# Summing the first experts' results: where the bias products, the residual rows and the last addition stand

## The chip, the cores and the metric

One core of one Trainium2 chip. The metric is the device time of a whole run in microseconds, as the median of several runs. All times inside a run are counted from the start of the profiled span.

## The reference

The program is two transformer blocks after one another on 512 tokens of width 1024. The first block ends in a mixture of 32 experts with 4 experts per token:

```python
y = act.astype(xb.dtype) @ w2[e] + b2[e]
...
out = jnp.zeros((T + 1, D), jnp.float32).at[buf_tok].add(ys.reshape(n_pad, D))[:T]
...
x = x + mod[:, 5] * moe_ffn(hf, *moe_w).reshape(B, L, D)
```

For each token: the four experts' outputs are multiplied by the token's gates and added, the experts' bias rows (`b_mlp2`) are added with the same gates, the sum is multiplied by a modulation row and added to the residual `x`. The second block starts from this `x`.

## The kernel before

A kernel is a chain of stages. Each stage (`stage(...)`) is a block in which the five engines run their own lists of instructions and meet at the end; the next stage begins when the last engine has arrived. Within a stage the order between engines is set by semaphores (`then_inc`, `wait_ge`).

The stage `combine1` is the function `combine`, called once by `expert_layer` after the first block's expert products. The 512 tokens are four tiles (`TX = 4`) of 128 tokens, one per partition, with 1024 columns. The work around the change:

- SyncE (SP) requests the 32 bias rows (`bias`, L2841), the modulation row on all partitions (`gate`, L2842), then the residual rows of the four tiles (`x_rows`, L2844), 128x1024 f32 each. In the kernel before they are requested at once, one after another.
- GpSimd (POOL) issues 16 gathers (L2851), tile by tile, four for each tile: gather j of tile t fetches, for every token of the tile, the output row of its j-th expert from `slot_rows` in HBM into `got[:, t, j]`. The first two of a tile count on `first[t]`, the last two on `rest[t]`.
- ScalarE turns gates into diagonal matrices (`shares`, L2880) and keeps the transposed gates (`spread_turned`, L2877).
- TensorE (PE) turns the gates (L2858). Then for each tile it multiplies them with the bias rows (L2864: two matmuls, shown as four instructions) and adds gathered rows 0 and 1 with the diagonal matrices (L2870: four matmuls, shown as eight instructions), all into two PSUM banks of the tile. All eight PSUM banks are in use, two for each tile. The last one signals `summed`.
- VectorE (DVE) adds gathered rows 2 and 3 (L2892, twice: the first reads PSUM, the second reads `total`), multiplies by `gate` (L2896) and adds the residual rows (L2898). `total` has two buffers, used in turn.

Behind it stands the stage `in2`, which begins with transposes of `x` on TensorE (L551), memsets on GpSimd (L3640) and the load of the first weights on SyncE (L147). The last stage of the program (`combine_last`, gathers at L2933, products at L2946) is built in the same way with two gathers for each tile and without residual rows.

Of the kernel before, what the change touches and what calls it, by code (L numbers as in the profile page):

```python
# [21 lines left out]
ALU = mybir.AluOpType  # L22
# [4 lines left out]
P = 128  # L27
D = 1024
DC = D // P
L = 512  # L30
LC = 256
TX = L // P
# [65 lines left out]
def record(**fields):  # L98

    return namedtuple("Record", list(fields))(**fields)  # L100
# [70 lines left out]
@contextmanager  # L171
def stage(core, name, *signals, pool_dma=(), from_one=()):

    nc = core.nc
    mine, other = core.halves[core.stages % 2], core.halves[1 - core.stages % 2]
    first = core.stages == 0
    core.stages += 1  # L180
    assert len(signals) <= len(mine)
    with ExitStack() as stack:  # L182
        found = {s: stack.enter_context(nc.semaphore(f"{name}_{s}", num=n)) for s, n in zip(signals, mine)}
        found.update({s: core.stack.enter_context(nc.semaphore(f"{name}_{s}")) for s in pool_dma})
        block = stack.enter_context(nc.Block(no_gpsimd_drain=True))
        if not first:
            @block.sync
            def _(sync):
                sync.sem_clear(range(other[0], other[-1] + 1))
        if from_one:  # L190
            @block.sync
            def _(sync):
                for signal in from_one:
                    sync.sem_inc(found[signal], 1)
        yield block, record(**found)


@contextmanager
def buffers(core, others=None, **shapes):

    with ExitStack() as stack:
        made = dict(others or {})
        for name, shape in shapes.items():
            kind = F32
            if not isinstance(shape[-1], int):
                *shape, kind = shape
            made[name] = stack.enter_context(core.nc.sbuf_tensor(f"{name}_{core.nc.next_id()}", list(shape), kind))
        yield record(**made)
# [24 lines left out]
def on_all(row, parts=P):  # L233

    return row.to_broadcast([parts, row.shape[1]])
# [2586 lines left out]
def combine(core, k, name, r, y_rows, rows, top, bias, x_rows):  # L2822

    psum = core.psum
    experts = bias.shape[0]
    by_tensor = top // 2
    with buffers(core, got=[P, TX, top, D], total=[P, 2, D], gate=[P, D], bias=[experts, D], spread_turned=[experts, L],
                 shares=[P, TX, by_tensor, P]) as b, \  # L2830
            stage(core, name, "gate_loaded", "added", "vector_step", "bias_loaded", "shares_turned", "shares_kept",
                  "spread_out", "summed", *[f"x{t}_loaded" for t in range(TX)],
                  pool_dma=("first0", "first1", "first2", "first3", "rest0", "rest1", "rest2", "rest3")) as (block, s):
        first = [s.first0, s.first1, s.first2, s.first3]
        rest = [s.rest0, s.rest1, s.rest2, s.rest3]
        sums_ps = psum[:, :, :].rearrange("p (t c) n -> p t (c n)", t=TX)
        x_loaded = [s.x0_loaded, s.x1_loaded, s.x2_loaded, s.x3_loaded]

        @block.sync
        def _(sync):  # L2840
            sync.dma_start(b.bias[:], bias).then_inc(s.bias_loaded, 16)  # L2841
            sync.dma_start(b.gate[:], on_all(rows[0:1, 5 * D:6 * D])).then_inc(s.gate_loaded, 16)  # L2842
            for t in range(TX):
                sync.dma_start(k.x[:, t], x_rows[t * P:(t + 1) * P, :]).then_inc(x_loaded[t], 16)  # L2844

        @block.gpsimd
        def _(pool):
            for t in range(TX):
                for j in range(top):
                    i = t * top + j  # L2850
                    pool.indirect_dma_start(b.got[:, t, j], None, y_rows,  # L2851
                                            bass.IndirectOffsetOnAxis(ap=r.dest[:, i:i + 1], axis=0))\
                        .then_inc(first[t] if j < by_tensor else rest[t], 16)

        @block.tensor
        def _(pe):
            for t in range(TX):
                mm = pe.transpose(psum[0:experts, 7, t * P:(t + 1) * P], r.shares[:, t, :], k.ident[:])  # L2858
            mm.then_inc(s.shares_turned, 1)
            pe.wait_ge(s.shares_kept, 1)  # L2860
            pe.wait_ge(s.bias_loaded, 16)
            for t in range(TX):
                for c in range(D // BANK):
                    pe.matmul(sums_ps[:, t, c * BANK:(c + 1) * BANK], b.spread_turned[:, t * P:(t + 1) * P],  # L2864
                              b.bias[:, c * BANK:(c + 1) * BANK], start=True, stop=False)
                pe.wait_ge(s.spread_out, t + 1)
                pe.wait_ge(first[t], 16 * by_tensor)
                for j in range(by_tensor):
                    for c in range(D // BANK):
                        mm = pe.matmul(sums_ps[:, t, c * BANK:(c + 1) * BANK], b.shares[:, t, j],  # L2870
                                       b.got[:, t, j, c * BANK:(c + 1) * BANK], start=False, stop=j == by_tensor - 1)
                mm.then_inc(s.summed, 1)

        @block.scalar
        def _(act):
            act.wait_ge(s.shares_turned, 1)
            act.copy(b.spread_turned[:], psum[0:experts, 7, :]).then_inc(s.shares_kept, 1)  # L2877
            for t in range(TX):
                for j in range(by_tensor):
                    ins = act.activation(b.shares[:, t, j], k.ident[:], ACT.Copy, scale=r.gates[:, t, j:j + 1])  # L2880
                ins.then_inc(s.spread_out, 1)
            act.wait_ge(s.spread_out, TX)

        @block.vector
        def _(dve):
            step = Steps(dve, s.vector_step)
            for t in range(TX):
                total = b.total[:, t % 2]
                dve.wait_ge(s.summed, t + 1)
                dve.wait_ge(rest[t], 16 * (top - by_tensor))  # L2890
                for j in range(by_tensor, top):
                    step(dve.scalar_tensor_tensor(out=total, in0=b.got[:, t, j], scalar=r.gates[:, t, j:j + 1],  # L2892
                                                  in1=sums_ps[:, t] if j == by_tensor else total, op0=ALU.mult, op1=ALU.add))
                if t == 0:
                    dve.wait_ge(s.gate_loaded, 16)
                step(dve.tensor_tensor(total, total, b.gate[:], ALU.mult))  # L2896
                dve.wait_ge(x_loaded[t], 16)
                dve.tensor_tensor(k.x[:, t], k.x[:, t], total, ALU.add).then_inc(s.added, 1)  # L2898
            dve.wait_ge(s.added, TX)


def combine_last(core, k, r, y_rows, gain, bias, out):
# [89 lines left out]
def expert_layer(core, k, args, which, router=None):  # L2992
# [13 lines left out]
    with buffers(core, logits=[P, TX, width], gates=[P, TX, top], dest=[P, TX * top, I32],  # L3006
# [39 lines left out]
        if first:  # L3046
            combine(core, k, "combine1", r, y_rows, k.rows1, top, args.b_mlp2[0], x_rows)
        else:
            combine_last(core, k, r, y_rows, args.ln2_g_2, args.ln2_b_2, args.out)
# [756 lines left out]
```

## Time and profile before

| | us |
|---|---|
| median of 3 runs | 2547.24 (2543.53 to 2547.29) |
| profiled execution, its own time | 2546.25 |
| span of the profiled execution | 2544.5 |
| mean granted TensorE clock | 0.909 |
| TensorE busy | 2161.3 (85%) |
| VectorE busy | 1025.3 (40%) |
| ScalarE busy | 734.6 (29%) |
| GpSimd busy | 268.7 (11%) |

Rows of the trace give times from the start of the span. `PE` is a matmul, `PEld` its weight load, `POOL` is GpSimd, `DVE` VectorE, `SP` SyncE; a row with xN merges N instructions of one line. The median and the span are not the same run: the profiled execution has its own time, 1.75 us above its span.

### The profile page before, as it was taken

To read this page: it belongs to the slowest core of one execution; us is meant where nothing else is said; L and a number is where in the kernel's file an instruction comes from. 1 tells how busy PE (TensorE), PEld (TensorE's weight loads), DVE (VectorE), ACT (ScalarE), POOL (GpSimd) and SP (SyncE) were. 2 spreads that over 40 slices of the span, in tenths; PEclk is the share of its full clock that TensorE was granted. 3 is DMA by queue.
4 is the path that set the end of the run, shared out by engine and by line. 5 is a ranking of instruction groups with operands and counts; after the bars stand their busy time and mean duration, and the time that the engine had idled before them with its cause. 6 is when DMAs were issued, how large, how long until landed. Compare 5 with 4: busy or idle time off the path is not lost. (4 is left out here: it accounts for less than half of the span.)

```text
span 2544.5 us, 43818 instructions
## 1 busy us (share of the span) xinstructions
PE 2161.3 (85%) x18094; PEld 1230.4 (48%) x18094; DVE 1025.3 (40%) x2002; ACT 734.6 (29%) x1874; POOL 268.7 (11%) x233
## 2 busy tenths in 40 slices
PE   5989779848998899889888887799989987793995
PEld 3965247733333344333333333488866644582442
DVE  3236546452222223222222221537246679545443
ACT  3223536321111111011101111235246677421322
POOL 0000000000000000000000000200059950000001
PEclk8999789969899999999999998899989996696997
DMA  6356620289799999999999995622000011302995
GB/s 237 109 205 251 253 90 1 77 362 416 306 421 421 420 421 419 420 421 420 421 421 420 420 410 237 251 85 83 34 2 1 1 68 67 141 17 88 418 418 199
DMA packets 147804, 628.05 MB, mean 247 GB/s; under 512 B 34516, under 2 KB 65492, under 8 KB 93848
## 3 DMA queue, kind: packets, MB, share of 16 engines
q1 hardware_dynamic: 118280, 575.56, 56.0%
q0 software_dynamic: 8064, 29.36, 2.9%
q10 hardware_dynamic: 21264, 20.34, 2.4%
q8 instruction: 143, 2.34, 0.4%
q14 instruction: 53, 0.43, 0.0%
HBM read 591.85 MB, written 33.38 MB: 246 GB/s over the span
## 5 line engine op out<-in xcount | busy, mean ns | idle before, releaser
L2292 PE MATMUL psum<-low,x 128*32 128x512 f32 x3520 | 416.9, 619 | 61.1 <-DMA low<-in_w_mlp 57.8
L2452 DVE TENSOR_TENSOR u<-psum,x 128x512 f32<-128x512 f32 x81 | 56.0, 691 | 690.9 <-PE psum L2292 690.9
L662 PE MATMUL psum<-high 128*128 128x512 f32 (+3 forms) x832 | 295.5, 355 | 19.2 <-DVE low L687 19.1
L662 PE MATMUL psum<-high,low 128*128 128x512 f32 (+3 forms) x832 | 293.3, 353 | 0.0
L662 PE MATMUL psum<-low,high 128*128 128x512 f32 (+3 forms) x832 | 293.2, 352 | 0.0
L2292 PEld LDWEIGHTS psum<-low,x 128*32 128x32 f32 x3520 | 113.4, 113 | 323.2 <-issue 234.3
L2301 PE MATMUL psum<-low,act_turned 128*32 128x256 f32 x4000 | 235.4, 387 | 3.9 <-DVE act_turned L2461 3.6
L2292 PE MATMUL psum<-high,x 128*32 128x512 f32 x1664 | 203.1, 628 | 37.2 <-DMA high<-in_w_mlp 31.9
L2301 PEld LDWEIGHTS psum<-low,act_turned 128*32 128x32 f32 x4000 | 132.7, 113 | 124.6 <-issue 51.8
L662 PEld LDWEIGHTS psum<-high 128*128 128x128 f32 x832 | 159.8, 192 | 42.4 <-issue 21.3
L2393 ACT ACTIVATE sig<-glu 128x256 f32<-128x256 f32 x81 | 34.5, 426 | 471.1 <-DVE glu L2453 470.8
L662 PEld LDWEIGHTS psum<-high,low 128*128 128x128 f32 x832 | 159.9, 192 | 21.4
L662 PEld LDWEIGHTS psum<-low,high 128*128 128x128 f32 x832 | 159.9, 192 | 20.9
L687 DVE TENSOR_TENSOR low<-weight_slots,high 128x1024 fp32r<-128x1024 f32 (+3 forms) x84 | 89.4, 1066 | 194.0 <-ACT high L681 193.3
L681 ACT CAST high<-weight_slots 128x1024 fp32r<-128x1024 f32 (+3 forms) x84 | 77.2, 920 | 216.1 <-PE psum L662 211.0
L2292 PEld LDWEIGHTS psum<-high,x 128*32 128x32 f32 x1664 | 52.8, 113 | 166.6 <-issue 113.2
L2384 ACT ACTIVATE x<-psum,cols,scale1f 128x128 f32<-128x128 f32 x160 | 58.0, 468 | 202.7 <-PE psum L2292 167.1
L2263 POOL DMA_INDIRECT x<-token_rows,slot_token x20 | 18.9, 946 | 889.8 <-PE psum L2283 868.6
L1229 ACT ACTIVATE weight_slots<-psum,shifts 128x768 f32<-128x768 f32 x96 | 86.6, 902 | 66.4 <-DVE shifts L1281 66.4
L355 PE MATMUL psum<-weight_slots,mix 128*32 128x512 f32 x384 | 58.9, 750 | 52.7 <-DMA weight_slots<-in_w_ada 28.4
L1280 DVE TENSOR_REDUCE peaks<-psum 128x1 f32<-128x768 f32 x96 | 91.5, 953 | 26.3 <-PE psum L1149 25.8
L2401 ACT COPY x<-psum 128x256 f32<-128x256 f32 x80 | 29.7, 372 | 239.2 <-DMA slot_rows<-x 149.5
(527 smaller groups left out, 3081.6 us busy)
## 6 DMA issues: line engine op xcount, KB each, us to landing
low<-in_w_mlp SPq DMA_DIRECT2D x141, 2048.0 KB, 27.2
high<-in_w_mlp SPq DMA_DIRECT2D x51, 2048.0 KB, 28.8
weight_slots<-in_w_ada SPq DMA_DIRECT2D x12, 2048.0 KB, 10.9
weight_slots<-in_w_mod SPq DMA_DIRECT2D x12, 2048.0 KB, 10.9
weight_slots<-in_w_in SPq DMA_DIRECT2D x8, 2048.0 KB, 8.4
gu<-in_w_gate SPq DMA_DIRECT2D x16, 1024.0 KB, 30.2
gu<-in_w_up SPq DMA_DIRECT2D x16, 1024.0 KB, 31.4
down<-in_w_down SPq DMA_DIRECT2D x16, 1024.0 KB, 31.4
```

Source lines behind the costliest of these rows:

```text
L355: mm = pe.matmul(out[c * 32:(c + 1) * 32], self.c[:, which, kp * self.KP + i, :], rows[:, i, c * BANK:(c + 1) * BANK], start=kp == 0 and i ...
L662: mm = pe.matmul(psum[:, p.group % 8, 0:p.width], *p.operands(x, weights[:, n % 2], u * QK_ + kc, kc), start=p.first and u == 0 and kc == ...
L681: act.copy(w.high[:, n % 2, :, 0:chunks[j].source.shape[2]], piece(j, u)).then_inc(s.high_made, 1)
L687: dve.tensor_tensor(w.low[at], piece(j, u), w.high[at].bitcast(F32), ALU.subtract).then_inc(s.low_made, 1)
L1229: act.activation(probs[c][:, t], rows_ps[t % 2], ACT.Exp, scale=scale, bias=b.shifts[:, c, t:t + 1], accum_out=b.sums[:, c, t:t + 1]).then ...
L1280: step(dve.tensor_reduce(b.peaks[:, c, t:t + 1], rows_ps[t % 2], AX, ALU.max))
L2292: mm = pe.matmul(psum[g * RB:(g + 1) * RB, bank, :], b.turned[:, kc, q * RB:(q + 1) * RB], w[:, i, g * BANK:(g + 1) * BANK], start=kc == 0 ...
L2301: mm = pe.matmul(psum[g * RB:(g + 1) * RB, 2 + parity, 0:YW], b.act_turned[:, parity, kc, :], w[:, i, g * YW:(g + 1) * YW], start=kc == 0, ...
L2384: ins = act.activation(b.turned[:, m, :], psum[:, 4 + m // 4, (m % 4) * P:(m % 4 + 1) * P], ACT.Identity, scale=k.scale1f[:, m:m + 1], bia ...
L2393: act.activation(b.sig[:], b.glu[:], ACT.Sigmoid, scale=ALPHA).then_inc(s.squashed, 1)
L2401: act.copy(b.y[:, q], psum[:, 2 + at % 2, 0:YW]).then_inc(s.y_kept, 1)
L2452: step.reach(dve.tensor_tensor(b.u[:], psum[:, bank, :], b.bias[:], ALU.add), s.biased, at + 1)
```

## The change

Three edits in `combine`. The bias products of all four tiles are issued before the first tile's gather products. SyncE requests the residual rows of tile t only when `rest[t]` has landed. The addition of `total` to the residual rows moves from VectorE to GpSimd, behind all its gathers; `total` gets a buffer for each tile, and a new semaphore, `totalled`, tells GpSimd that a tile's total is ready.

```diff
-    with buffers(core, got=[P, TX, top, D], total=[P, 2, D], gate=[P, D], bias=[experts, D], spread_turned=[experts, L],
+    with buffers(core, got=[P, TX, top, D], total=[P, TX, D], gate=[P, D], bias=[experts, D], spread_turned=[experts, L],
                  shares=[P, TX, by_tensor, P]) as b, \
-            stage(core, name, "gate_loaded", "added", "vector_step", "bias_loaded", "shares_turned", "shares_kept",
+            stage(core, name, "gate_loaded", "added", "totalled", "vector_step", "bias_loaded", "shares_turned", "shares_kept",
...
             for t in range(TX):
+
+                sync.wait_ge(rest[t], 16 * (top - by_tensor))
                 sync.dma_start(k.x[:, t], x_rows[t * P:(t + 1) * P, :]).then_inc(x_loaded[t], 16)
...
                         .then_inc(first[t] if j < by_tensor else rest[t], 16)
+            for t in range(TX):
+                pool.wait_ge(x_loaded[t], 16)
+                pool.wait_ge(s.totalled, t + 1)
+                pool.tensor_tensor(k.x[:, t], k.x[:, t], b.total[:, t], ALU.add).then_inc(s.added, 1)
+            pool.wait_ge(s.added, TX)
...
                     pe.matmul(sums_ps[:, t, c * BANK:(c + 1) * BANK], b.spread_turned[:, t * P:(t + 1) * P],
                               b.bias[:, c * BANK:(c + 1) * BANK], start=True, stop=False)
+            for t in range(TX):
                 pe.wait_ge(s.spread_out, t + 1)
                 pe.wait_ge(first[t], 16 * by_tensor)
...
-                total = b.total[:, t % 2]
+                total = b.total[:, t]
...
-                step(dve.tensor_tensor(total, total, b.gate[:], ALU.mult))
-                dve.wait_ge(x_loaded[t], 16)
-                dve.tensor_tensor(k.x[:, t], k.x[:, t], total, ALU.add).then_inc(s.added, 1)
-            dve.wait_ge(s.added, TX)
+                dve.tensor_tensor(total, total, b.gate[:], ALU.mult).then_inc(s.totalled, 1)
+            dve.wait_ge(s.totalled, TX)
```

## Rows read from the trace of the kernel before

**Rows 1.** The page, its first line.

```profile
span 2544.5 us, 43818 instructions
```

**Rows 2.** Timeline of the stage: start us, us, engine, line, instructions [idle before, releaser].

```profile
1586.50 0.94 POOL L2851 DMA_INDIRECT got<-slot_rows,dest  x1 [85.41 <-POOLq L182]
...
1588.37 3.75 PE L2864 MATMUL psum<-bias,spread_turned 32*128 32x512 f32 x4 [1.51 <-DMA bias<-in_b_mlp]
...
1597.30 5.66 PE L2870 MATMUL psum<-got,shares 128*128 128x512 f32 x8 [5.18 <-DMA got<-slot_rows,dest]
...
1602.89 1.98 PE L2864 MATMUL psum<-bias,spread_turned 32*128 32x512 f32 x4
...
1605.14 1.27 POOL L2851 DMA_INDIRECT got<-slot_rows,dest  x1 [0.30 <-issue]
...
1615.88 3.70 PE L2870 MATMUL psum<-got,shares 128*128 128x512 f32 x8
...
1619.62 1.28 DVE L2892 SCALAR_TENSOR_TENSOR total<-got,gates,psum 128x1024 f32<-128x1024 f32 x1 [0.42 <-PE psum L2870]
...
1623.51 1.23 DVE L2898 TENSOR_TENSOR x<-x,total 128x1024 f32<-128x1024 f32 x1
...
1625.34 3.53 PE L551 MATMUL psum<-ident,x 128*128 128x128 f32 x16 [5.76 <-PEq L182]
```

**Rows 3.** The same stage by line: duration ns min/median/max, first and last start us.

```profile
L2864 PE MATMUL psum<-bias,spread_turned x16: 587/588/1188, 1588.4 to 1615.4; 32*128 32x512 f32 x16
...
L2892 DVE SCALAR_TENSOR_TENSOR total<-got,gates,total x4: 1284/1284/1285, 1604.3 to 1620.9; 128x1024 f32<-128x1024 f32 x4
L2896 DVE TENSOR_TENSOR total<-total,gate x4: 1224/1224/1225, 1605.6 to 1622.3; 128x1024 f32<-128x1024 f32 x4
```

**Rows 4.** Windows of 2 us: busy us (count) by engine, PEclk, DMA share, GB/s.

```profile
1590.00:1592.00 2.00, 2.00 (x3) 0.33 (x1) 0.00 (x0) 0.00 (x0) 1.47 (x2) 0.50 1.00 381
...
1614.00:1616.00 2.00, 2.00 (x6) 0.75 (x6) 1.88 (x2) 0.00 (x0) 0.00 (x0) 1.00 0.83 330
```

**Rows 5.** DMA from 1580 to 1630: the gathers' queue, then issues (median us to landing).

```profile
q0 software_dynamic: 2304, 8.39, 42.1%
...
x<-x_rows SPq DMA_DIRECT2D x4, 512.0 KB, 9.0
...
bias<-in_b_mlp SPq DMA_DIRECT2D x1, 128.0 KB, 2.3
```

**Rows 6.** Landing of the gathers in this stage (L2851), then L2933 in the last stage.

```profile
DMA to landing us min/median/max: 8.1/11.6/11.8
...
L2933 POOL DMA_INDIRECT got<-slot_rows,dest x8: 936/938/941, 2510.9 to 2519.6; - x8
...
DMA to landing us min/median/max: 6.1/6.3/7.6
```

**Rows 7.** Windows of 1 us around a rise and a fall of the clock (columns as rows 4).

```profile
1600.00:1601.00 1.00, 1.00 (x3) 0.48 (x2) 0.00 (x0) 0.00 (x0) 0.84 (x1) 0.50 1.02 410
1601.00:1602.00 1.00, 1.00 (x4) 0.43 (x3) 0.00 (x0) 0.00 (x0) 0.69 (x2) 0.84 1.02 406
...
1621.00:1622.00 1.00, 0.00 (x0) 0.00 (x0) 1.00 (x1) 0.00 (x0) 0.00 (x0) 0.90 0.00 0
```

**Rows 8.** The gathers' queue from 2514 to 2515, last stage: packets, MB.

```profile
q0 software_dynamic: 28, 0.11, 30.9%
```

**Rows 9.** GpSimd's two-input operations, and VectorE's beside them: min/median/max ns.

```profile
L1109 POOL TENSOR_TENSOR acc<-acc,part x36: 1812/1832/1847, 1875.6 to 2050.6; 128x772 f32<-128x772 f32 x36
...
L3283 POOL TENSOR_TENSOR weighted<-xs,to_end x10: 1899/1902/2883, 2071.3 to 2101.5; 128x1024 f32<-128x1024 f32 x10
...
L3352 DVE TENSOR_TENSOR skipped<-xs,skip x2: 2918/2938/2957, 2071.3 to 2074.2; 128x1024 f32<-128x1024 f32 x2
...
L3362 DVE TENSOR_TENSOR h<-h,whole x16: 684/692/2424, 2081.7 to 2112.4; 128x512 f32<-128x512 f32 x16
...
L3364 DVE TENSOR_TENSOR h<-h,psum x16: 686/686/689, 2082.5 to 2113.2; 128x512 f32<-128x512 f32 x16
```

## The prediction

> **What bounds the kernel now.** I read the page first. One core runs for 2544.5 us [rows 1], and the profiled execution's own time, 2546.25 us, is 1.75 us above that. The change touches one stage, `combine1`, so I went on to the timeline of that stage. It opens with the gathers at 1586.5, its last addition (L2898) ends at 1624.7, and TensorE's next stage begins at 1625.34 [rows 2]: 39 us, 1.5% of the span. Nothing before the stage changes, and everything after it starts when it ends. So the question is when the last addition ends.
>
> Three streams run in it. **TensorE**: the timeline shows four bias products (L2864) and eight gather products (L2870) per tile, the last set at 1615.88, with nothing between [rows 2]; from 1602.9 it is never idle, and VectorE takes tile 3 at 1619.62, when the last product is summed. A tile costs TensorE 5.54 us: L2864 begins a tile at 1602.89, and after three such steps, 1602.89 + 3 x 5.54 = 1619.5, tile 3 is summed. **VectorE** needs 1.28 + 1.28 + 1.22 + 1.23 us for a tile [rows 2, 3], 5.1 with the gaps between, so it waits 0.4 us per tile for TensorE. **DMA** is the stream that the page's averages hide: by windows it is full from 1590 to about 1615.7 at 380 to 410 GB/s [rows 4, 7]. It moves 16 gathers of 512 KB (8.39 MB), four residual tiles of 512 KB and the gate and bias rows [rows 5]. At 410 GB/s a 512 KB tile costs 1.28 us; GpSimd issues a gather every 1.245 us (16 issues from 1586.50 to 1605.14 [rows 2]). Issue rate and transfer rate are nearly equal, so whatever else is transferred delays the gathers by its size. That is why a gather lands 11.6 us after its issue here, but 6.3 us after it in the last stage, which requests no residual rows [rows 6]. So TensorE sets the end, with DMA some 4 us ahead of it (1615.7 against 1619.5).
>
> **The change, part by part.**
>
> *Bias products at the head.* Twelve of the 16 L2864 instructions move ahead of tile 0's products. Before, TensorE sits idle from 1592.1 until the gathers land at 1597.30 [rows 2]. Four bias products take 3.75 us at the half clock and 1.98 at the full one [rows 2]; with the last of a set taking 1.19 or 0.59 us [rows 3], a step is 0.85 or 0.46 us. [...] With the same delay the bias run from 1588.37 has five slow steps (4.3 us) and eleven fast ones (5.1 us less the pause of 0.1 between sets: 4.8), and ends near 1597.4. Lower bound, full clock at once: 16 x 0.44, 1595.4; upper bound, never: 16 x 0.85, 1602.0. Against the 1597.3 at which tile 0 now starts this costs nothing. Eight gather products take 3.70 us, 3.6 of it before the next set, so tiles 1 to 3 lose 5.54 - 3.6 = 1.9 us each, and tile 0, now at a half clock for most of its 5.66 us [rows 2], 2.0: TensorE alone could sum tile 3 at 1597.4 + 4 x 3.6 = 1611.8, 7.7 us earlier.
>
> *Residual rows behind the gathers.* The first gather's packets start 3.5 us after its issue in the last stage (0.11 MB moved from 2514 to 2515, first issue at 2510.9 [rows 6, 8]). So packets start near 1590.0, tile 0's first pair is in at about 1590.0 + 2.56 + 0.5 = 1593.1, and the bias run, not the gathers, holds tile 0. But SyncE now requests tile t's rows when `rest[t]` has landed: rows of tiles 0, 1 and 2 still enter among later gathers, 1.28 us each. All the bytes except tile 3's residual still precede the last gather. Packets end at 1615.7 now, so the last gather's end at 1615.7 - 1.28 = 1614.4. Check from the front: 1590.0 + 19 x 1.28 = 1614.3. The semaphore comes a little later, between 0 and 1.2 us (1605.14 + 11.8 against 1615.7); I take 0.5. `rest[3]` is then 1614.9, and `first[3]`, two gathers earlier, 1612.3. In the same way `first[1]` is 1599.5, `first[2]` 1606.0. TensorE: tile 0 to 1601.0, tile 1 to 1604.6, tile 2 waits and goes 1606.0 to 1609.7, tile 3 waits again and goes 1612.3 to 1616.0 (3.7 us [rows 2]). So of TensorE's 7.7 us only 3.5 remain: the DMA takes the rest.
>
> Tile 3's residual is requested at 1614.9. 128 KB takes 2.3 us from issue to landing [rows 5]; with 0.96 us more to move it is 3.3, so 1618.2. Worst row: 9.0 us under load [rows 5], 1623.9. SyncE has nothing else queued behind its four waits, and the gathers stand ahead of the additions on GpSimd, so no wait delays an issue.
>
> *The addition by GpSimd.* VectorE loses 1.23 us per tile. No GpSimd addition of this shape is in the trace. Nearest: L1109, two full inputs, 128x772, 1832 ns; L3283, 128x1024 with a spread-out second input, 1902 ns [rows 9]. By size L1109 gives 1832 x 1024 / 772 = 2430 ns; bounds 1.90 and 2.43. I take 2.4, since both inputs are full. On the path, behind the last gate product, that is 1.15 us more than now.
>
> *Do the two engines get in each other's way?* L3352, a VectorE product of two SBUF tensors beside L3283, takes 2.94 us, though one of that size takes 1.22 alone (L2896); L3362, 128x512, takes 0.69 at best and 2.42 at worst; L3364, of equal size but with a PSUM input, is always 0.69 [rows 3, 9]. I read: a VectorE operation with two SBUF tensors waits out a GpSimd addition, or the reverse; one with PSUM doesn't. [...] By that rule the sum below gives 1.3, and without any exclusion it would give 2.3.
>
> Per tile VectorE has one free step (L2892 from PSUM) and two exposed ones. GpSimd's last gather issue ends at 1606.4, so addition 0 starts no earlier. Step by step: VectorE tile 0 1601.0 to 1604.9; tile 1: PSUM step to 1606.2, second to 1607.5; addition 0 from 1607.5 to 1609.9; tile 1's gate product to 1611.1. Addition 1 to 1613.5 while tile 2's PSUM step runs; tile 2's second step to 1614.8, gate product to 1616.1. Addition 2 to 1618.5; tile 3 PSUM step 1616.1 to 1617.4, second step 1618.5 to 1619.8, gate product to 1621.0. Addition 3 (rows in at 1618.2) to 1623.4. Now: 1624.7. **Gain 1.3 us**, so 2543.2 us of span, and 2545.0 as its own time. The median of the three runs, 2547.24, is 1.0 above the profiled one, so I forecast 2545.9.
>
> *Descriptors.* The last gather issue takes 1.27 us instead of 0.94, beside VectorE steps with two SBUF inputs [rows 2, 3]. VectorE now works during four issues, so up to 4 x 0.33 = 1.3 us; by then a gather's backlog is about 3 us (landing 9.8 after issue against 6.3), which hides it. Without that backlog it would land on the end in full.
>
> **Rivals.**
> 1. *No mutual exclusion here*: VectorE tile 3 runs 1616.0 to 1619.9, addition to 1622.3: gain 2.3 us; own time 2543.9, median 2544.9. For: L1109's 36 times vary by 0.03 us [rows 9]. Against: L3352.
> 2. *TensorE's clock falls in a gap.* After tile 3's last product at 1619.6 the clock stays full until about 1621.9, 2.3 us, then is half [rows 7]. The gap that I foresee ahead of tile 3 is 2.6 us. If it falls, eight products take 7 x 0.85 + 1.19 = 7.2 us instead of 3.7: tile 3 summed at 1619.5, VectorE 1623.4, addition 1625.8: **1.1 us slower** than now; median 2548.3. Below a gap of some 2.3 us it has nothing to stand on.
> 3. *The late residual is the new end.* If tile 3's rows take 9.0 us, the addition runs 1623.9 to 1626.3, 1.6 us slower; median 2548.8. Against: the queue is empty by then. It decides from a landing later than 1621.0.
> 4. *Residual rows don't delay the gathers.* Then TensorE sums tile 3 by 1612; without the exclusion VectorE ends at 1601.0 + 4 x 3.9 = 1616.6, the addition at 1619.0: gain 5.7 us, median 2541.5. With it the alternation above still ends at 1623.4. Against: DMA at its ceiling [rows 4].
> 5. *The clock never rises in the stage*: bias to 1602.0, four tiles of 6.9 us to 1629.6, end at 1636: 11 us slower, median 2558. Against: the rise at 1601.3.
>
> **How the numbers follow.** My case 0.48, rival 1 0.20, rival 2 0.17, rival 3 0.09, rival 4 0.04, rival 5 0.02. 0.2%, or 5.1 us, is about what a measurement of this kernel can tell from no change. Only rivals 4 and 5 reach it. Runs of one kernel spread 3.8 us (2543.53 to 2547.29), which adds some chance on both sides: faster 0.07, same 0.87, slower 0.06. Range: rivals 1 to 3 span 2544.9 to 2548.8; with that spread and part of rival 4, 2542.0 to 2549.5. The addition's lower bound, 1.90 us, shortens each turn of the alternation and gives 1621.7, a gain of 3.0: inside too.
>
> **What would show it.** L2864 16 times in one run from 1588.4, ending near 1597.4; the DMA full until about 1614.5, with 0.5 MB after it; L2870 starting after waits for `got` at tiles 2 and 3, a full clock at tile 3; the addition on GpSimd at 2.4 us; VectorE's second L2892 or its gate product lengthened towards 2.4 to 3.6 us wherever an addition runs; the next stage's first matmul at about 1624.0. I am wrong if an addition costs over 3 us, if gathers land before 1610 (then the rows cost no bandwidth), or if a stage outside this one moves.

## Result, and the profile after

The changed kernel is slower. Median 2558.14 us (2553.83 to 2559.9, 6 runs) against 2546.33 us (2543.39 to 2552.55, 6 runs of the kernel before): ratio 1.0038, 95% interval 1.0023 to 1.0052, that is 6 to 13 us, or about 0.4%. I had forecast 2545.9, a gain of 1.3.

The profiled execution takes 2557.54 us and spans 2555.8. It reaches the changed stage 1.4 us later than the kernel before did, so I count from the stage's first gather (1587.86 here, 1586.50 in [rows 2]). The timeline of the stage in the changed kernel:

```profile
1589.87 13.99 PE L2871 MATMUL psum<-bias,spread_turned 32*128 32x512 f32 x16 [1.65 <-DMA bias<-in_b_mlp]
...
1603.79 16.74 PE L2878 MATMUL psum<-got,shares 128*128 128x512 f32 x32
...
1606.48 0.94 POOL L2853 DMA_INDIRECT got<-slot_rows,dest  x1 [0.30 <-issue]
1610.26 1.28 DVE L2900 SCALAR_TENSOR_TENSOR total<-got,gates,psum 128x1024 f32<-128x1024 f32 x1 [33.92 <-PE psum L2878]
...
1612.90 1.22 DVE L2904 TENSOR_TENSOR total<-total,gate 128x1024 f32<-128x1024 f32 x1
1614.04 1.27 DVE L2900 SCALAR_TENSOR_TENSOR total<-got,gates,psum 128x1024 f32<-128x1024 f32 x1
1614.28 2.36 POOL L2859 TENSOR_TENSOR x<-x,total 128x1024 f32<-128x1024 f32 x1 [6.86 <-DVE total L2904]
1615.35 2.37 DVE L2900 SCALAR_TENSOR_TENSOR total<-got,gates,total 128x1024 f32<-128x1024 f32 x1
1617.76 1.23 DVE L2904 TENSOR_TENSOR total<-total,gate 128x1024 f32<-128x1024 f32 x1
...
1628.80 2.34 POOL L2859 TENSOR_TENSOR x<-x,total 128x1024 f32<-128x1024 f32 x1 [2.49 <-DVE total L2904]
...
1631.59 3.65 PE L551 MATMUL psum<-ident,x 128*128 128x128 f32 x16 [11.06 <-PEq L182]
```

Beside [rows 2]: the stage, first gather to the next stage's first matmul, takes 43.7 us instead of 38.8. The 16 bias products take 13.99 us: 16 steps at the half clock (0.50), as four of them took 3.75. TensorE then works without a pause, and no gather is waited for. VectorE gets tile 0 at 1610.26, 22.4 us after the first gather; before it was 16.5. The windows of 1 us (columns as rows 4) show why:

```profile
1603.00:1604.00 1.00, 1.00 (x3) 0.22 (x2) 0.00 (x0) 0.00 (x0) 0.69 (x2) 0.50 1.01 406
...
1608.00:1609.00 1.00, 1.00 (x2) 0.34 (x1) 0.00 (x0) 0.00 (x0) 0.00 (x0) 0.50 1.03 410
1609.00:1610.00 1.00, 1.00 (x3) 0.52 (x2) 0.00 (x0) 0.00 (x0) 0.00 (x0) 0.83 1.00 397
1610.00:1611.00 1.00, 1.00 (x4) 0.46 (x3) 0.74 (x1) 0.00 (x0) 0.00 (x0) 1.00 1.06 422
```

TensorE is busy without a break from 1589.9, and its granted clock is still at the half level 19 us later. It rises at 1609.3, which is 5.5 us after the first *gather* product.

The DMA, the addition and VectorE's steps went as forecast. Two-us windows of the DMA, and the lines of the addition and of VectorE's steps (min/median/max ns):

```profile
1614.00:1616.00 2.00, 2.00 (x6) 0.88 (x5) 1.97 (x3) 0.00 (x0) 1.72 (x1) 1.00 0.99 397
1616.00:1618.00 2.00, 2.00 (x6) 0.95 (x5) 1.97 (x2) 0.00 (x0) 0.64 (x1) 1.00 0.11 43
```

```profile
L2859 POOL TENSOR_TENSOR x<-x,total x4: 2337/2348/2362, 1614.3 to 1628.8; 128x1024 f32<-128x1024 f32 x4
```

```profile
L2900 DVE SCALAR_TENSOR_TENSOR total<-got,gates,psum x4: 1273/1273/1281, 1610.3 to 1623.7; 128x1024 f32<-128x1024 f32 x4
L2900 DVE SCALAR_TENSOR_TENSOR total<-got,gates,total x4: 1285/2348/2373, 1611.6 to 1625.0; 128x1024 f32<-128x1024 f32 x4
```

The DMA is full until about 1616.1, 28.2 us after the first gather (forecast 27.9). An addition takes 2.35 us. VectorE's second step takes 1.285 us beside nothing and 2.35 beside an addition; the step that reads PSUM takes at most 1.281 us, beside an addition too. VectorE and GpSimd alternate at 4.84 us per tile. But VectorE gets tile 0 22.4 us after the first gather instead of the forecast 14.5, and the last addition ends after 43.3 us (1631.1) instead of 36.9.

The stage explains 4.9 us of the 11.3 between the spans of the two profiles. 1.4 lie ahead of it, where nothing differs, and 5.0 behind it: from L551 to the end it is 924.2 us instead of 919.2. That part has its own experiments below.

### The profile page after: what moved, and what is told of

It is laid out like the page before. It is cut to its first block and busy times, and to the rows that moved or that the text cites. A ratio compares the mean times of both kernels' runs of the same rounds, so it can differ in the third digit from the quotient of the medians.

```text
span 2555.8 us, 43819 instructions
## 1 busy us (share of the span) xinstructions
PE 2168.5 (85%) x18094; PEld 1231.5 (48%) x18094; DVE 1024.5 (40%) x1998; ACT 734.3 (29%) x1874; POOL 277.7 (11%) x237
## 5 line engine op out<-in xcount | busy, mean ns | idle before, releaser
L2301 PEld LDWEIGHTS psum<-low,act_turned 128*32 128x32 f32 x4000 | 131.3, 112 | 123.2 <-issue 48.8
## 6 DMA issues: line engine op xcount, KB each, us to landing
weight_slots<-in_w_ada SPq DMA_DIRECT2D x12, 2048.0 KB, 10.8
```

What stands on the lines that cost most here:

```text
L2301: mm = pe.matmul(psum[g * RB:(g + 1) * RB, 2 + parity, 0:YW], b.act_turned[:, parity, kc, :], w[:, i, g * YW:(g + 1) * YW], start=kc == 0, ...
```

## The experiments

"Stage" below is always the time from the first gather (L2851 of the kernel before) to the first matmul of the next stage (L551) in the profile; "behind" is from there to the end of the span, "ahead" is all before the first gather.

**The three parts of the change, one at a time.** First the bias products alone:

```diff
                     pe.matmul(sums_ps[:, t, c * BANK:(c + 1) * BANK], b.spread_turned[:, t * P:(t + 1) * P],
                               b.bias[:, c * BANK:(c + 1) * BANK], start=True, stop=False)
+            for t in range(TX):
                 pe.wait_ge(s.spread_out, t + 1)
```

> The kernel before with only the 16 bias products moved to the head of TensorE's list. Theory A (the clock): the granted clock stays at its half level through the run of bias products, 13.7 us, and through tile 0's products; tile 0 is summed about 6 us later than in the kernel before, and since VectorE then needs 5.1 us for each of four tiles the stage ends about 5 us later; the run is 4 to 6 us slower. Theory B (the cost of the change is the alternation of VectorE and GpSimd, the clock does not matter): no change, within 1 us.

Stage 42.7 us, 3.9 more than the 38.8 of [rows 2]. Bias run and gather products in its timeline, and the clock around the rise:

```profile
1586.24 13.99 PE L2864 MATMUL psum<-bias,spread_turned 32*128 32x512 f32 x16 [2.14 <-DMA bias<-in_b_mlp]
...
1600.16 16.49 PE L2871 MATMUL psum<-got,shares 128*128 128x512 f32 x32
```

```profile
1603.00:1604.00 1.00, 1.00 (x3) 0.48 (x2) 0.00 (x0) 0.00 (x0) 0.73 (x1) 0.50 1.06 422
1604.00:1605.00 1.00, 1.00 (x2) 0.27 (x2) 0.00 (x0) 0.00 (x0) 0.00 (x0) 0.71 1.03 397
1605.00:1606.00 1.00, 1.00 (x4) 0.50 (x3) 0.00 (x0) 0.00 (x0) 0.00 (x0) 1.00 1.01 406
```

The same picture without the other two edits: half clock through the run, a rise 4.4 us into the gather products. Over 12 runs the time is 1.0010 (0.9996 to 1.0024) of the kernel before: the sign is as expected, but the interval holds both the 4 us of theory A and no change. The profile decides for A, not the total.

Then the residual rows alone (the `wait_ge` on `rest[t]` ahead of each request):

> The kernel before with only the residual rows requested tile by tile behind rest[t]. Theory A: the gathers of tile 0 land about 4 us earlier, TensorE keeps its order and its clock, its last product ends 3 to 4 us earlier and so does the stage: 3 us faster. Rival (the late residual rows are the cost): VectorE waits for tile 3's rows, requested only when the last gather has landed, and the stage ends where it did or 1 to 2 us later.

Stage 36.6 us, 2.2 less; 0.9992 (0.9978 to 1.0005) over 12 runs. Tile 0's products start 7.5 us after the first gather instead of 10.8. VectorE waits once for the rows, 0.6 us for tile 2, so the rival is there but small. Theory A's 3 us were not reached: the clock rose 6.1 us into tile 0's products instead of 4.0, and the eight took 6.68 us instead of 5.66. This edit is the only one of the three that shortens the stage.

The addition alone (GpSimd, `total` for each tile; bias products and requests as before):

> The kernel before with only the last addition on GpSimd, one total buffer for each tile. Theory A: a GpSimd addition of 2.36 us in place of 1.23 us stands behind the last tile, and VectorE's second step waits it out at most in part, because TensorE hands over a tile only every 5.54 us: 1 to 1.5 us slower. Theory B: VectorE and GpSimd alternate from the first tile and the stage ends 4 us or more later.

Stage 39.3 us, 0.5 more; 1.0005 (0.9989 to 1.0021). TensorE hands over a tile every 5.54 us, so the additions mostly fall beside VectorE's idle time and no second step is lengthened by more than 0.03 us. Tile 0 was summed 0.6 us earlier here than in [rows 2]; from VectorE's first step for tile 3 to the next stage it is 6.8 us instead of 5.7, the 1.1 us that theory A gives to the slower addition. Theory B is out: the alternation costs little by itself.

And the changed kernel with the bias products back in each tile:

> The changed kernel with the bias products back at the head of each tile. Theory A: TensorE's clock rises some 4 us after tile 0's first gather product, tile 0 is summed near 1600 instead of 1610, and the stage is 6 to 8 us shorter than in the changed kernel, 1 to 2 us shorter than in the kernel before. Theory B: the stage is as long as in the changed kernel. Theory C (a part of the loss comes from code or data placement of the later stages): the loss behind the stage, about 5 us, stays.

Stage 37.6 us, 6.1 less than the changed kernel and 1.2 less than before; 0.9996 (0.9981 to 1.0011) over 12 runs, against 1.0038 for the changed kernel. The loss inside the stage is the place of the bias products. The part behind is 918.9 us in this profile, so theory C, as code or data placement, finds no support here; how little one profile says of that part is shown in the last of these experiments.

**Why doesn't the clock rise during the bias products?** They differ from the gather products in one visible thing: both operands are 32 rows deep (`32x512`) instead of 128. So they were made 128 deep, with the sums unchanged (only the buffers, the wait and the filling are shown; e6 fills `bias` with 1.0, e7 with 0.0):

```diff
-    ... bias=[experts, D], spread_turned=[experts, L],
+    ... bias=[P, D], spread_turned=[P, L],
...
+            pe.wait_ge(s.padded, 4)
...
+            for at in (slice(32, 64), slice(64, 128)):
+                dve.memset(b.spread_turned[at], 0.0).then_inc(s.padded, 1)
+                dve.memset(b.bias[at], 1.0).then_inc(s.padded, 1)
```

> The changed kernel with the bias products made 128 rows deep: rows 32 to 127 of the bias tile are 1.0 and those of the gates 0.0, written by VectorE at the stage's head; the sums are the same. Theory A1 (products that fill 32 of the 128 rows don't bring the clock up): the clock rises 4 to 6 us into the bias run, the run takes 10 us instead of 14, tile 0 is summed near 1601 to 1603 by the time of the kernel before, and the stage is 6 us shorter than in the changed kernel (about 37.5 us). Rival A2 (the clock stays low for another reason, such as the pause before the stage or the products' order): the run takes 14 us again and the stage stays at 43 to 44 us.

> As the kernel with 128-row bias products, but the added rows are 0.0 in both operands. Theory A1 (rows in use count, whatever they hold): as there, clock up 4 to 6 us into the run, stage about 37.5 us. Rival A3 (what counts is the data that toggle): the clock stays at half through the run and the stage is at 43 to 44 us.

With ones: run 8.94 us instead of 13.99, stage 38.0. With zeros in both operands: run 9.07 us, stage 37.4. Timeline of the one with zeros, and its windows:

```profile
1585.77 9.07 PE L2872 MATMUL psum<-bias,spread_turned 128*128 128x512 f32 x16 [2.96 <-DVE bias L2898]
...
1594.67 7.03 PE L2879 MATMUL psum<-got,shares 128*128 128x512 f32 x16
...
1598.31 1.28 DVE L2904 SCALAR_TENSOR_TENSOR total<-got,gates,psum 128x1024 f32<-128x1024 f32 x1 [12.69 <-PE psum L2879]
...
1602.25 3.67 PE L2879 MATMUL psum<-got,shares 128*128 128x512 f32 x8 [0.55 <-DMA got<-slot_rows,dest]
...
1608.66 3.67 PE L2879 MATMUL psum<-got,shares 128*128 128x512 f32 x8 [2.74 <-DMA got<-slot_rows,dest]
```

```profile
1588.00:1589.00 1.00, 1.00 (x2) 0.34 (x1) 0.00 (x0) 0.00 (x0) 0.76 (x1) 0.50 0.99 352
1589.00:1590.00 1.00, 1.00 (x3) 0.39 (x2) 0.00 (x0) 0.00 (x0) 0.94 (x1) 0.64 0.93 307
```

The clock rises 3.9 us into the run (3.7 in the other). Both A2 and A3 fall: with the same order and as long a pause ahead, and whether the added rows hold ones or zeros, the clock rose once the products were 128 rows deep. Apart from the depth there are only the four fillings on VectorE, which let the run begin 2.9 us after the first gather instead of 2.0. This is also close to the schedule that I had forecast for the change: tile 2's and tile 3's products wait for `got` (0.55 us, forecast 1.4, and 2.74 us, forecast 2.6), and the stage takes 37.4 us where the forecast was 38.8 - 1.3 = 37.5. Totals: 0.9979 (0.9965 to 0.9992, 9 runs) with ones and 0.9998 (0.9985 to 1.0011, 11 runs) with zeros. The two do the same work, and by the profiles the one with ones has the longer stage, yet its total is the lower one by 0.2%. So a difference of that size can come out of such totals without a cause.

The one with ones shows rival 2 as well. After the pause ahead of tile 3 the clock falls and comes back:

```profile
1611.00:1612.00 1.00, 1.00 (x3) 0.46 (x3) 1.00 (x1) 0.00 (x0) 1.00 (x1) 1.00 1.03 410
1612.00:1613.00 1.00, 1.00 (x2) 0.34 (x1) 1.00 (x1) 0.00 (x0) 0.20 (x1) 0.54 1.03 414
...
1615.00:1616.00 1.00, 1.00 (x3) 0.16 (x1) 0.00 (x0) 0.00 (x0) 1.00 (x1) 0.76 0.50 106
```

```profile
1610.81 5.37 PE L2879 MATMUL psum<-got,shares 128*128 128x512 f32 x8 [2.73 <-DMA got<-slot_rows,dest]
```

Tile 3's eight products take 5.37 us instead of 3.67, and the stage 0.6 us more. With an equal pause of 2.7 us the clock fell in this profile and not in the one with zeros, nor in the next version below (e9), where the pause was 2.7 us too.

**A version built from the parts.** The kernel before, with rows behind the gathers, 128-row bias products for tiles 0 and 1 ahead of tile 0's products and those of tiles 2 and 3 one step behind, and the addition on VectorE:

```diff
+            bias_products(0)
+            bias_products(1)
             for t in range(TX):
...
                 mm.then_inc(s.summed, 1)
+                if t + 2 < TX:
+                    bias_products(t + 2)
```

> The kernel before with residual rows behind the gathers, 128-row bias products (zeros in the added rows), those of tiles 0 and 1 ahead of tile 0's gather products and those of tiles 2 and 3 one step behind, and the addition left on VectorE. Theory A: the clock is up before tile 0's products, tile 0 is summed 12 us after the first gather, VectorE's four tiles of 5.03 us no longer set the end, tile 3's pair lands at 25.8 us and is summed at 29.5, and the stage takes 35 to 36 us: 3 us shorter than before, 8 shorter than in the changed kernel. Theory B': the late residual rows of tile 3 hold VectorE and the stage is as long as with the rows moved alone, 36.6 us.

Stage 36.0 us. Over 12 runs 2545.07 against 2547.69 us, 0.9988 (0.9976 to 1.0000) of the kernel before, where the changed kernel has 1.0033 to 1.0038: clearly better than the changed kernel, and against the kernel before at the edge of what can be told. Half of B' is true. VectorE waits for the rows at each of tiles 0 to 2 (1.14, 0.78 and 1.37 us), since a tile's rows are requested only with its last gather, and with the addition on VectorE that wait stands in the chain.

**What lies behind the stage.** The changed kernel once more, with runs of both kernels on one chip:

> The changed kernel once more, unchanged, on the chip of this call. Theory A (the clock, inside the stage): the stage is 43 to 44 us from its first gather to the next stage's first matmul, 5 us longer than before; the 5 us that the first profile shows behind the stage don't come back, and over many runs the kernel is about 5 us slower than before, not 11. Theory C (the later stages are slowed by the change): the later stages are again 5 us longer and the whole is 10 us slower.

Stage 43.2 us, behind 927.6. 2557.55 (11 runs) against 2548.88 us (26 runs), 1.0033 (1.0022 to 1.0044): 6 to 11 us. So the total loss is larger than the stage's, against theory A taken alone. Four further executions, one profile each:

> The kernel before once more, one look. It shows how far the stages behind the combine stage move from one execution to another with no change at all. Theory A: the part behind the stage differs from the first profile's by up to 5 us or more, as much as the changed kernel's did. Theory C: it agrees with the first profile's within 1 us.

> The kernel before, one more look. Theory C0 (the two forms of the carry stage, 44.8 and 48.7 us from its first GpSimd product to its last matmul, come with any kernel by chance): in these two looks of the kernel before at least one shows the longer form, or the run stays near 2543 with the shorter one. Theory C1 (the change brings the longer form): both looks show the shorter form again, as the first two did.

> The kernel before, one more look, with the same question as the look ahead of it.

> The changed kernel, a third look. All theories: the combine stage takes 43 to 44 us. Theory C0: the carry stage may show either form. Theory C1: the longer form a third time.

and, since e11 had shown a longer part behind for the kernel before, and e12 once more for the changed one, a bare delay (four multiplications on VectorE behind the last addition, on a buffer that nothing reads) and three more executions:

> The kernel before with four more VectorE multiplications of 1.26 us at the end of the combine stage, on a buffer that nothing reads afterwards: the next stages start 5.0 us later and nothing else changes. Theory C0 (the later stages don't care when they start; their longer forms come by chance): 5 us slower over many runs. Theory C2 (a combine stage that ends 5 us later meets the later stages at another moment of the clock, and they take their longer forms more often): 8 to 10 us slower, as the changed kernel is, with the longer form of the carry stage in the profile.

> The kernel before, one more look. C0: either form of the carry stage. C1 (the change brings the longer form): the shorter form.

> The kernel before, one more look. C0: either form of the carry stage. C1 (the change brings the longer form): the shorter form.

> The changed kernel, a fourth look. The combine stage takes 43 to 44 us. C0: the carry stage may show either form. C1: the longer form again.

| execution | ahead | stage | behind | carry stage |
|---|---|---|---|---|
| before (first profile) | 1586.5 | 38.8 | 919.2 | 44.8 |
| before, e8 | 1583.1 | 38.7 | 919.5 | 44.8 |
| before, e10 | 1586.5 | 39.0 | 919.4 | 44.8 |
| before, e11 | 1579.3 | 40.2 | 923.7 | 48.7 |
| before, e14 | 1585.6 | 38.8 | 919.3 | 44.7 |
| before, e15 | 1585.8 | 39.2 | 926.0 | 48.7 |
| changed (first profile) | 1587.9 | 43.7 | 924.2 | 48.7 |
| changed, e5 | 1587.2 | 43.2 | 927.6 | 48.8 |
| changed, e12 | 1589.1 | 43.9 | 928.2 | 48.6 |
| changed, e16 | 1578.5 | 43.6 | 924.3 | 48.7 |
| before with delay, e13 | 1586.9 | 44.2 | 924.1 | 48.8 |

The carry stage lies in the second block, some 445 us after the first matmul of the next stage. It is counted from the first start of L3283 on GpSimd to the last start of L3300 on TensorE (L3289 and L3306 in the changed kernel). By line, e8, then e11, then the changed kernel:

```profile
L3283 POOL TENSOR_TENSOR weighted<-xs,to_end x10: 1899/1902/2884, 2067.7 to 2097.9; 128x1024 f32<-128x1024 f32 x10
...
L3300 PE MATMUL psum<-h,raw x32: 592/592/697, 2081.9 to 2112.5; 128*128 128x512 f32 x32
```

```profile
L3283 POOL TENSOR_TENSOR weighted<-xs,to_end x10: 1897/1901/2883, 2065.6 to 2098.5; 128x1024 f32<-128x1024 f32 x10
...
L3300 PE MATMUL psum<-h,raw x32: 592/592/1091, 2080.8 to 2114.3; 128*128 128x512 f32 x32
```

```profile
L3289 POOL TENSOR_TENSOR weighted<-xs,to_end x10: 1899/1902/2882, 2078.3 to 2111.3; 128x1024 f32<-128x1024 f32 x10
...
L3306 PE MATMUL psum<-h,raw x32: 592/592/1061, 2093.6 to 2127.0; 128*128 128x512 f32 x32
```

It has two forms, 3.9 us apart, with no code changed between them: the same kernel shows the short one four times and the long one twice. In the long form TensorE begins L3300 about a microsecond later and meets a half clock (maximum 1061 to 1193 instead of 697 ns). The rows just ahead of it, e8 and then e11:

```profile
2078.11 0.71 DVE L3362 TENSOR_TENSOR h<-h,whole 128x512 f32<-128x512 f32 x1 [0.29 <-PE psum L3310]
...
2081.90 1.98 PE L3300 MATMUL psum<-h,raw 128*128 128x512 f32 x4 [1.60 <-DVE h L3364]
```

```profile
2075.30 2.42 DVE L3362 TENSOR_TENSOR h<-h,whole 128x512 f32<-128x512 f32 x1 [0.91 <-PE psum L3310]
...
2080.80 3.54 PE L3300 MATMUL psum<-h,raw 128*128 128x512 f32 x4 [3.75 <-DVE h L3364]
```

In e11 VectorE's first L3362, which reads two SBUF tensors, starts 0.03 us after a GpSimd product and takes 2.42 us instead of 0.71, TensorE pauses 3.75 us instead of 1.60, and its granted clock is at half from 2081.1 to 2084.5, for nearly all of L3300's first four products. In all twelve profiles with the long form, those of the parts included, this pause is 3.7 to 3.8 us and the clock falls; in all six with the short form it is 1.6 us and the clock stays up. What decides which form an execution takes isn't shown.

The changed kernel shows the long form four times in four. On average the stage is 43.6 against 39.1 us (4.5 more) and the part behind 926.1 against 921.2 us (4.9 more), which together give 9.4 us, near the 8.7 between the medians of e5's runs. The part ahead, which no edit touches, moves between 1578.5 and 1589.1 us in this table, more than either of the other two parts, so the total of a single execution says little. The delay kernel has a stage of 44.2 us and the long form; over 12 runs it is 1.0019 (1.0007 to 1.0031) of the kernel before, 2 to 8 us slower with a median 7 us higher. C0's 5 us lie in that interval, C2's 8 at its edge and its 10 outside. C1, that the change alone brings the long form, had e8, e10 and e14 for it and fell with e11 and e15. Four of four and one of one against two of six is too little to tell whether it brings it more often. The other kernels don't order the forms by the length of the stage either: the stages of 37.6 and 37.4 us (bias per tile, zeros) came with the short form, those of 36.0, 36.6, 38.0, 39.3 and 42.7 us (e9, e2, e6, e3, e1) with the long one, and e3, whose stage is as long as before to within 0.5 us, has the longest part behind of all, 928.3 us. Whether the change makes the long forms more frequent stays open.

## Why the prediction was wrong

- **What bounds it now**: right. TensorE sets the stage's pace before the change, 5.54 us a tile, and the residual rows do delay the gathers: their median landing is 11.6 us after the issue in the kernel before and 8.0 with the rows moved alone (e2), which gave 2.2 us.
- **Bias products at the head**: this is the step that failed. In the kernel before the granted clock is 0.50 when tile 0's first gather product starts at 1597.30 and rises at about 1601.3, 4.0 us later [rows 2, 7]. "With the same delay the bias run from 1588.37 has five slow steps (4.3 us) and eleven fast ones" took the rise 4.0 us into tile 0's *gather* products [rows 7] for a rise 4.0 us into any work. No run shows that term of 9.0 us for products 32 rows deep. Measured: sixteen slow steps, 14.0 us, a little more than the 13.6 of the upper bound that I gave and then left out of the sum. And I let the clock be up for tile 0's products, which took 6.5 us instead of 3.6. The two together, with the bias DMA's landing 0.1 us later, put tile 0 7.9 us late. The last addition ends 6.4 us late and not 7.9, because the first addition, which the forecast let wait for GpSimd's last gather issue, begins 4.0 us after VectorE takes tile 0 instead of 6.5.
- **The same step, the evidence at hand**: [rows 2] had the warning. Four bias products ran at 3.75 us from 1588.37, and 9 us later the gather products started at the half clock again. That could still be put down to the shortness of the run; no row of before showed a long run of 32-row products from a low clock, so the term of 9.0 us should have been carried into the range with its upper bound *and* a slow tile 0. The 4.0 us was one value too: in the other profiles here, of bias products 32 rows deep, the clock rises 3.0 (e3) to 6.1 us (e2) after the first gather product.
- **Residual rows**: right in size (full DMA until 28.2 us after the first gather, forecast 27.9; shortest landing of a tile's rows 3.3 us, as forecast). The 9.0 us that I called the worst is the median of before; the longest was 12.1. But the edit was worthless in the changed kernel, where TensorE comes to every tile later than the tile's gathers do: its 32 gather products run from 1603.79 without a wait for `got`, and in e1, without this edit, they run so too. That is why the parts don't add up: 3.9 - 2.2 + 0.5 = 2.2 us alone, 4.9 together.
- **Addition by GpSimd**: right, 2.35 us for a forecast 2.4.
- **Mutual exclusion**: right. VectorE's second step, which reads two SBUF tensors, takes 2.35 us beside an addition instead of 1.285, the step that reads PSUM at most 1.281 us, and rival 1 is out. The exclusion costs next to nothing where TensorE hands over a tile every 5.54 us (e3: no second step over 1.308 us), and it sets the pace of 4.84 us per tile where the tiles stand ready.
- **Descriptors**: didn't matter. VectorE was idle while the gathers were issued, and the last issue took 0.94 us, as the others did; in the kernel before it took 1.27.
- **Rivals**: 2 was seen in one kernel (e6), where the clock came back after 3.4 us and the stage lost 0.6 us; 3 and 4 are out. 5, the clock that never rises, was the nearest to what happened, at 0.02. It had the right cause for the bias run, too low a chance, and too high a price, since the clock does rise 4 to 6 us into the gather products. That the median it named, 2558, is the measured one is luck: it put 11 us into the stage, which lost 4.9, and the rest of the measured loss lies elsewhere.
- **The range**: its upper end, 2549.5, rested on the 3.8 us spread of three runs. The 94 runs of the kernel before that these experiments brought, in four groups, reach from 2540.3 to 2559.5 us. And no case priced anything behind the stage; I only named it as a sign of being wrong.

## What to carry to other kernels

A row that shows when the clock rises holds for the kind of product that ran: ask how many rows deep a moved product is before giving it a fast step. Here 13.99 us of 32-row products passed without a rise, and in 128-row ones it came after 3.9 us. Work pulled into an idle gap is free only as long as it fits the gap at the clock it will really get; here the 16 products of 32 rows ended 16.0 us after the first gather, where tile 0's gather products had started at 10.8. Padded to 128 rows with zeros (e7) a product takes 593 ns at the full clock instead of 588, the run begins 0.9 us later and takes 9.07 us instead of 13.99. And a transfer moved behind others pays only where the consumers of those others had been waiting for them: the residual rows alone gave 2.2 us, where TensorE had waited 5.18 us for tile 0's gathers, and had nothing to give in the changed kernel, where it waited for none, as in e1 without that edit. Move the one whose wait the profile names first.

## What the hardware showed unexpectedly

- Matmuls of 32 rows kept TensorE busy for 14.0 us with the granted clock at 0.50 throughout, in five profiles of two kernels. In every one the clock rose 4.4 to 5.7 us after the first gather product, which is 128 rows deep. The same products padded to 128 rows, with zeros or ones in the added rows of `bias`, saw it rise after 3.9 and 3.7 us. Depths between 32 and 128 were not tried.
- At the full clock a 32-row product takes as long as a 128-row one (medians of 588 and 592 ns, L2864 and L2870 in the kernel before). From the half clock the two kinds still differed, with no rise in 13.99 us of the one and a rise after 3.9 us of the other: equal durations did not mean an equal effect on the clock.
- Two executions of the same kernel can differ by 4 us in one stage: with a pause of TensorE of 1.6 us ahead of L3300 the clock stayed up (697 ns at most for a product), with 3.7 to 3.8 us it fell to half (1061 ns and more), in 18 profiles without exception.
